# Delta rule in a hybrid block: 32x32 blocks joined by single block products; norm roots and two gate outputs moved on ScalarE

## The reference

```python
u = rms_norm(h)
proj = einsum(u, w_in)            # attention q,k,v; delta q,k,v; out-gate; beta; decay; two branch gates
y_a = differential_attention(...) # per-head RMSNorm of the result
# delta rule, per chunk and head, A strictly lower triangular:
A = where(strict, einsum('bhnid,bhnjd->bhnij', k * beta, k) * decay, 0)
T = inverse(I + A)                # unit lower triangular solve against I
v_new = T @ (v * beta) - (T @ (k * beta * exp(gc))) @ S
o = (q * exp(gc)) @ S + (q @ k.T * decay) @ v_new
S = S * g_tot + k_dec.T @ v_new
y_d = rms_norm(o) * silu(gate)
mixed = sigmoid(gate_a) * (y_a @ w_branch_attn) + sigmoid(gate_d) * (y_d @ w_branch_dn)
h = h + mixed @ w_out
h = h + hierarchical_moe(rms_norm(h))   # 32 experts, top-1 group, top-2 experts
out = rms_norm(h)[meta:]
```

## Time and profile before

| | |
|---|---|
| median of 3 runs | 659.19 us (658.57 to 659.19) |
| profiled execution: its own time | 658.39 us |
| profiled execution: span | 656.7 us |
| granted TensorE clock, mean | 0.968 |
| TensorE busy | 601.6 us (92%) |
| VectorE busy | 326.4 us (50%) |
| ScalarE busy | 267.8 us (41%) |
| GpSimd busy | 55.2 us (8%) |

### The profile page before, as it was taken

How to read it: one execution, slowest core, us unless ns; L and a number is a source line. 1 busy time by engine, 2 the same in 40 slices (tenths; PEclk the granted TensorE clock), 3 DMA queues, 4 the chain that set the end, 5 groups by cost and what they waited for, 6 DMA issues and landing times.

```text
span 656.7 us, 14323 instructions
## 1 busy us (share of the span) xinstructions
PE 601.6 (92%) x5931; PEld 505.6 (77%) x5931; DVE 326.4 (50%) x693; ACT 267.8 (41%) x598; POOL 55.2 (8%) x102
## 2 busy tenths in 40 slices
PE   8999999999999799999999999999999778686985
PEld 8999999989998788999899999997554533444551
DVE  5344467888877558465756389534122111110103
ACT  6245566777778545324533575423110010000103
POOL 8300011110000002100310030000000000000000
PEclk9899999999999899999999999999999988896989
DMA  9745443434335233222421169999999999999993
GB/s 289 242 146 179 151 144 99 138 119 135 122 126 191 66 129 130 66 66 65 130 66 66 65 225 347 420 422 416 421 421 419 421 422 423 422 422 421 421 405 129
DMA packets 68560, 156.04 MB, mean 238 GB/s; under 512 B 4818, under 2 KB 54116, under 8 KB 56596
## 3 DMA queue, kind: packets, MB, share of 16 engines
q1 hardware_dynamic: 67136, 154.89, 62.7%
q0 software_dynamic: 176, 0.17, 0.2%
q10 hardware_dynamic: 1188, 0.12, 0.2%
HBM read 154.12 MB, written 1.05 MB: 236 GB/s over the span
## 4 chain that ended last, share of the span: by engine, by line
PE 67%; DMA 8%; DVE 8%; SPq 7%; ACT 6%; issue 3%; ACTq 0%; DVEq 0%
PE bank L861 33%; DMA arena<-in_expert_w_gate_dram 8%; PE bank L1272 7%; SPq L526 7%; PE bank L1048 5%; PE bank L846 3%; PE bank L1297 2%; PE bank L1253 2%; PE bank L1026 2%; PE bank L1308 2%; DVE ring_lo L341 1%; PE bank L929 1%; ACT w_hi L336 1%; DVE arena L1921 1%; ACT arena L1572 1%
## 5 line engine op out<-in xcount | busy, mean ns | idle before, releaser
L861 PE MATMUL bank<-uT_hi,w_hi 128*128 128x272 f32 (+1 forms) x568 | 169.5, 298 | 3.4 <-ACT arena L1441 3.4
L861 PE MATMUL bank<-uT_hi,ring_lo 128*128 128x272 f32 (+1 forms) x568 | 163.4, 288 | 0.0
L861 PE MATMUL bank<-uT_lo,w_hi 128*128 128x272 f32 (+1 forms) x568 | 163.3, 288 | 0.0
L341 DVE TENSOR_TENSOR ring_lo<-arena,w_hi 128x1024 fp32r<-128x1024 f32 x88 | 107.6, 1225 | 49.0 <-ACT w_hi L336 48.8
L861 PEld LDWEIGHTS bank<-uT_hi,w_hi 128*128 128x128 f32 x568 | 108.6, 191 | 6.2 <-ACT w_hi L336 3.9
L861 PEld LDWEIGHTS bank<-uT_lo,w_hi 128*128 128x128 f32 x568 | 108.7, 191 | 0.2 <-issue 0.2
L861 PEld LDWEIGHTS bank<-uT_hi,ring_lo 128*128 128x128 f32 x568 | 108.6, 191 | 0.0
L336 ACT ACTIVATE w_hi<-arena 128x1024 fp32r<-128x1024 f32 x88 | 92.0, 1051 | 0.9 <-DMA arena<-in_w_in_dram 0.9
L1272 PE MATMUL bank<-arena 128*32 128x256 f32 x1024 | 67.6, 423 | 20.9 <-DMA arena<-in_expert_w_gate_dram 20.9
L1272 PEld LDWEIGHTS bank<-arena 128*32 128x32 f32 x1024 | 35.5, 121 | 47.8 <-issue 26.9
L1921 DVE SCALAR_TENSOR_TENSOR arena<-arena 128x272 f32<-128x272 f32 x72 | 35.9, 498 | 12.3 <-ACT arena L1434 11.6
(11 more groups left out here) (368 smaller groups left out, 1011.7 us busy)
## 6 DMA issues: line engine op xcount, KB each, us to landing
arena<-in_w_in_dram SPq DMA_DIRECT2D x36, 1024.0 KB, 5.2
arena<-in_expert_w_gate_dram SPq DMA_DIRECT2D x32, 1024.0 KB, 24.9
arena<-in_expert_w_up_dram SPq DMA_DIRECT2D x32, 1024.0 KB, 21.8
arena<-in_expert_w_down_dram SPq DMA_DIRECT2D x29, 1024.0 KB, 22.0
arena<-in_w_branch_attn_dram SPq DMA_DIRECT2D x4, 1024.0 KB, 5.2
arena<-in_w_branch_dn_dram SPq DMA_DIRECT2D x4, 1024.0 KB, 5.1
arena<-in_w_out_dram SPq DMA_DIRECT2D x4, 1024.0 KB, 8.3
arena<-in_expert_w_down_dram SPq DMA_DIRECT2D x6, 512.0 KB, 18.3
```

Source lines behind the costliest of these rows:

```text
L341: nc.vector.tensor_tensor(low_of(SPLIT[q]), src, w_hi[HI_OF[q]].bitcast(F32), ALU.subtract).then_inc(w_lo_ready, 1)
L861: last = pe.matmul(ps[:, 0:b.shape[2]], a[:, c, :], b[:, c, :], start=(c == 0 and i == 0), stop=(c == NC - 1 and i == 2))
```

## The change

In the delta rule, each joined pair of 32x32 blocks is now one product of 32x32 blocks, in its own tile of the array. x2 multiplies A's blocks straight from `w[1]` by T's block, the result going to the rows of the lower block (tiles (0,32) and (64,96), 8 products per chain); VectorE multiplies it by the key factor on its way out of PSUM (it was ScalarE's copy). t2 makes the lower product for rows 32 to 63 in tile (32,32), and the two transposed ones in tiles (32,0) and (96,64), 12 products per chain; VectorE copies three 32x32 blocks for the four heads to their places. ScalarE copies T's transposed diagonal to `w[0]` in t1. GpSimd's mask `off64_c` and its multiply go.

On ScalarE, `roots` follows `key_roots` at once, with the table load left at its old place behind the first meta step; and the outputs of the first two gate tiles in the mix (gate+2, gate+3) stand ahead of the splits beside them, on VectorE too.

```diff
{DIFF}
```

More of the change, by code:

```diff
@@ L17 @@
 Q = P // 2
+B = P // 4
 META = 16
@@ L129, in hybrid_block @@
         block16 = new(P)
-        ident_c, block16_c, off32_c, off64_c = (new(Q) for _ in range(4))
+        ident_c, block16_c, off32_c = (new(Q) for _ in range(3))
+        new(Q)
         tri16, causal_add16, spread16 = (new(P) for _ in range(3))
@@ L459, in diagonal, with rows32 @@
             return a[q * Q:(q + 1) * Q, :, q * Q:(q + 1) * Q]
+        def rows32(i):
+            return slice(i * B, (i + 1) * B)
         every, first_half, rest = slice(None), slice(0, H // 2), slice(H // 2, H)
@@ L489, in hybrid_block @@
                     BEHIND.append(("split", n))
+                elif steps_seen == 1:
+                    BEHIND.insert(-1, ("tile", n))
                 else:
@@ L701, in _ @@
                     link(pool.memset(off32_c[half, 32 * b:32 * b + 32], 1.0))
-                link(pool.tensor_scalar(off64_c[rows, :], off32_c[rows, :], -1.0, 1.0, ALU.mult, ALU.add))
                 link(pool.tensor_tensor(off32_c[rows, :], off32_c[rows, :], block16_c[rows, :], ALU.subtract))
@@ L764, in dn @@
                     wait_dn(pool, "act", t, c, "at")
-                    pool.tensor_tensor(small(c, 4, 0), small(c, 6, 1), off32_c.unsqueeze(1).broadcast_to([P, 4, Q]), ALU.mult)
-                    pool.tensor_tensor(small(c, 4, 1), small(c, 6, 1), off64_c.unsqueeze(1).broadcast_to([P, 4, Q]),
+                    pool.tensor_tensor(small(c, 4, 0), small(c, 6, 1), off32_c.unsqueeze(1).broadcast_to([P, 4, Q]),
                                        ALU.mult).then_inc(dn_pool[c], 1)
@@ L1041, in dn, with both @@
                 Xs, Ys, Zs = (bank[2 + 3 * c + i][:, 0:4 * Q].rearrange("p (h i) -> p h i", h=4) for i in range(3))
-                def both(o, lhsT, rhs, quarters=(0, 1)):
+                def both(o, lhsT, rhs):
                     for h in range(n):
-                        for q in quarters:
+                        for q in range(2):
                             rows = slice(q * Q, (q + 1) * Q)
@@ L1121, in dn @@
                     need("dve", "t32")
-                    both(Zs, small(c, 4, 1), T)
+                    for h in range(n):
+                        for i in (0, 2):
+                            pe.matmul(Zs[rows32(i + 1), h, 0:B], w[1][rows32(i), h, rows32(i + 1)], T[rows32(i), h, 0:B], start=True, stop=True,
+                                      tile_position=(i * B, (i + 1) * B))
                     last = each(Y, kT, lambda h: S[:, 4 * c + h, :])
                 elif s == "t2":
-                    need("act", "x2")
-                    both(Zs, TT_, X_, (0,))
-                    last = both(Xs, X_, TT_)
+                    need("dve", "x2")
+                    for h in range(n):
+                        pe.matmul(Zs[rows32(1), h, 0:B], TT_[rows32(1), h, B:Q], X_[rows32(1), h, 0:B], start=True, stop=True,
+                                  tile_position=(B, B))
+                        for i in (1, 3):
+                            last = pe.matmul(Xs[rows32(i - 1), h, 0:B], X_[rows32(i), h, 0:B], TT_[rows32(i), h, B:Q], start=True, stop=True,
+                                             tile_position=(i * B, (i - 1) * B))
                 elif s == "x3":
@@ L1531, in roots @@
                 act.activation(rs_halves, rs_rows, ACT.Copy).then_inc(rs_ready, 1)
-                act.preload_act_table_set("exp_and_others")
             for m in range(FIRST_SLOT, SLOTS_A):
@@ L1595, in dn @@
                         done(act.activation(small(c, 5, 1), Xs, ACT.Copy))
-                elif s == "x2":
-                    wait_dn(act, "pe", t, c, s)
-                    done(act.activation(small(c, 5, 0), Zs, ACT.Copy))
+                elif s == "t1":
+                    wait_dn(act, "dve", t, c, "t32")
+                    for q in range(2):
+                        last = act.activation(diagonal(w[0], q), small(c, 5, 1)[q * Q:(q + 1) * Q], ACT.Copy)
+                    done(last)
                 elif s == "v":
@@ L1617, in _ @@
             key_roots()
+            roots()
             for what, arg in BEHIND:
                 if what == "roots":
-                    roots()
+                    act.preload_act_table_set("exp_and_others")
                 elif what == "split":
@@ L2064, in dn @@
                     of_pe()
+                    done(tt(piece(5, 0)[:, :, 0:B], Zs[:, :, 0:B], per_head(nbk, B), ALU.mult))
                     for h in range(n):
@@ L2069, in dn @@
                     of_pe()
-                    tt(T[0:Q], Zs[0:Q], T[0:Q], ALU.add)
-                    for q in range(2):
-                        rows = slice(q * Q, (q + 1) * Q)
-                        last = tt(diagonal(b(0), q), Xs[rows], piece(5, 1)[rows], ALU.add)
+                    dve.tensor_copy(T[rows32(1), :, 0:B], Zs[rows32(1), :, 0:B])
+                    wait_dn(dve, "act", t, c, "diag")
+                    for i in (0, 2):
+                        last = dve.tensor_copy(b(0)[rows32(i), :, rows32(i + 1)], Xs[rows32(i), :, 0:B])
                     done(last)
```

4 lines of the change are left out of this document (2 added, 2 removed).

## The result

The kernel with the change takes **655.55 us** (median of 16 runs, 649.6 to 657.3), the one before, on the same chip, 658.83 us (median of 16, 654.84 to 663.05). The ratio is 0.9942, with the interval 0.9919 to 0.9966; it lies near the ratio of the two means (0.9944), and that of the two medians would be 0.9950. The profiled execution took 656.16 us, its span is 654.4 us: 2.2 and 2.3 less than those of before.

What follows compares the result with a forecast made beforehand. The expert weight stream bounds the kernel from 392 us, and earlier TensorE savings start it sooner. From 658.39 us, less 0.5 (stall) and 1.8 (products), 656.1; with the median 0.8 higher, 656.9 us, range 654.9 to 659.1.

Steps and rivals of the forecast that it cites:

- The bound, and where a saving counts: From 392 us the expert weight stream sets the pace; TensorE time saved before about 390 us comes off one for one.
- product term: Smaller products in x2 and t2 of the delta rule, four times in all, save 1.8 us on TensorE's path.
- The stall: Before gate+4, about 217 us: wait falls from 3.36 to 0.6 us, 2.7 us returns before s2; 0.5 us kept.
- Rival 4: The stall before gate+4 goes altogether as VectorE reaches L2023 in time; 653.0 us, chance 0.04.
- The clock: Behind the stall the clock likeliest falls again to 1.2 GHz, costing about 1.6 us as before, so no term.
- the middle between 1.1 and 2.5: Saving on x2 and t2 taken as 1.8 us, between a 30.6 ns pass floor (1.1) and continued column scaling (2.5).
- the two products of rows 32 to 63 go one after another: In t2, these take 16 passes at 31 ns, 0.49 us, the third product beside them; 0.51 us saved against 1.0.
- the upper end: In x2 and t2 time goes with the columns: 0.24 and 0.51 us saved, times four 3.0 us.
- rival 3: In x2 and t2 the 32x32 tiles stop overlapping, 3.1 us lost; 661.8 us in all, chance 0.1.
- Rival 2: In x2 and t2 narrower products are no cheaper, only the stall's 0.5 us stays; 658.7 us, chance 0.16.
- Edits at nothing: Copies and multiplies moved or added on ScalarE, VectorE and GpSimd in x2, t1 and t2 cost TensorE nothing.
- The sum: Whole kernel: profiled 658.39 us less 0.5 and 1.8 is 656.1; with the median 0.8 higher, 656.9 us.

Runs made afterwards that it cites:

- e3_s1_first: The changed kernel with the meta chunk's s1 moved ahead of the splits on ScalarE, VectorE and GpSimd; 653.66 us, ratio 0.993 to the kernel before.
- e5_by_tile: The changed kernel with t2's products ordered tile by tile, four heads in each, instead of taking the tiles in turn; one run, 656.19 us.
- e9_alternate: The kernel before with t2's three 64x64 products head by head, tile (64,64) between the two of tile (0,0); t2 2.00 us as before, span 659.4 us.
- e7_again: The changed kernel, unchanged, profiled a second time; one run, 650.94 us.
- e6_compact: The changed kernel with s1 and s2 moved early and all products of delta-rule steps s1 to t1 made as 32x32 blocks; 659.26 us, ratio 1.0009 to before.

## Why the prediction was right, and where it was not

**The bound, and where a saving counts: right.** (One row was misread: 20.9 us is what TensorE's four waits for gate weights take together, the longest is 6.5 us. The bound is the same.) The stretch at 415 GB/s kept its length, the stream began 4.35 us earlier, and the leads at `t2` and behind it were kept up to 390 us. The time of 655.55 us lies inside the range. It is 1.35 us below the forecast of 656.9, about the 0.2% that a measurement tells. The main reason is the product term, which was 1.9 us short.

**The stall: right in place and size.** Gate+4 was forecast at 217.63 with 0.6 us of idle time and stood at 217.52 with 0.52. L2039 (before: L2023) was forecast at 221.24 and started at 221.07, `s2` at 221.72 and started at 221.34. The term was 0.5 us, and the trace gives 0.9 at `s2` and 0.6 at chunk 0. `e3_s1_first` shows that the cause was VectorE's order: with `s1` ahead of the splits the wait at `s2` is gone. Rival 4, by which the whole stall of 3.4 us goes, failed on just this.

**The clock: right in price, not a matter of one answer.** The fall costs 1.5 us, where 1.6 was taken. The step "the likeliest case has the clock fall again" held in the changed kernel's first profile and failed in its second, so that taking one of the two was a guess that the first profile happened to bear out. I had taken idle time as what decides. It doesn't alone: 0.52 and 2.16 us of it went both ways.

**The product term was mis-sized: 1.8 us taken, 3.7 measured.** The step that failed is the choice of the middle between 1.1 and 2.5, and within the bounds the sentence "the two products of rows 32 to 63 go one after another". For `x2` the upper end was exact: 0.24 us saved per chain. A pass of 32x32 blocks holds its tile for 31 ns, so the time in a tile does go with the columns from 128 (111 ns) to 64 (60) to 32 (31). For `t2` I gave the rows 32 to 63 to one pass at a time. They are two tiles, (32,32) and (32,0), and all three tiles ran beside each other: 0.63 us for both chains instead of 1.0 at my upper end. The real upper end was four times 0.24 and twice 1.37. I had seen that the two products now differ in their columns of the array, and used it only for the bad side, in rival 3.

**The rivals on the product.** Rival 2 (no cheaper) and rival 3 (tiles stop overlapping) are both refuted by 0.37 and 0.63 us. `e5_by_tile` shows that overlap is worth 0.5 us per chunk, and `e9_alternate` that it can't be had without the smaller blocks. The Trainium skill's rule in "TensorEngine Tiling (Array Packing)", on instruction overhead, of about 60 cycles for each matmul, by which rival 2 would have held, doesn't agree with this trace if it is read in columns: passes in one tile go from about 60 ns to 31 as the columns halve. Read as a time, 60 cycles at the 2.4 GHz level are 25 ns by an estimate, less than either, and the trace doesn't speak against it within a tile. The floor of about 25 ns between small matmuls, in the Trainium skill's "TensorE: Matmul & The Clock Gate", the part on the back-to-back issue gap, doesn't hold across tiles here: 48 passes in 0.63 us are 13 ns each, and within a round they start 7 ns apart. In one tile they start 31 ns apart, above it.

**Edits at nothing: right.** ScalarE's four copies in `t1` (1.71 us from 280.33) ended at 282.04 and L1453 started at 282.06, against 282.37 for L1441; all of it has moved 0.6 us earlier, so the pairs delayed it by some 0.3 us and TensorE didn't notice. A pair took 0.86 us, where I had put 0.64. VectorE's new multiply took 0.29 us, and its copies in `t2` 0.28 us each. TensorE shows no wait for any of them.

**The sum.** By the terms as measured, 3.7 and 0.6, and with the same base of 659.19, it would have been 654.9; the measured ratio's interval, on 658.83, is 653.5 to 656.6. The forecast of 656.9 lies 0.3 us outside it. The 0.6 us holds with the clock fallen as in before; where it stays up, as in `e7_again`, TensorE is 1.5 us further ahead. As 654.9 is the range's lower end, it took some luck that the result lies inside it.

## What to carry to other kernels

Where small products stand on the path, look for blocks of zeros in them: a product cut down to its 32x32 blocks cost half the time of a 64x64 one in its tile, and tiles that share rows but not columns still ran side by side, if the order takes them in turn. But count the instructions: the same cut applied to all steps, with twice the instructions in them, left TensorE idle for 10.1 us with nothing awaited that the profile shows, and took the whole gain. And when a wait is taken away by moving one engine's work, read on that engine's timeline what stands in front of the next operand. Here the gain of 2.8 us at one tile was 0.9 us one step later, and it took more moves, on three steps, to keep it.

## What the runs showed of the hardware that I had not expected

- Tiles (32,32) and (32,0) of the array, the same rows with different weights, overlap in the changed kernel: rounds of three passes start about 31 ns apart, 13 ns per pass over `t2`.
- Passes in different tiles start out of the order of the program. In `e5_by_tile`, L1140's first pass starts at 287.13, after five of the eight passes of L1136 that stand ahead of it. In the changed kernel's `t2` one pass of L1136 and two of L1139 alternate, so it seems that a product's second pass comes after the first passes of its neighbours.
- TensorE can idle with nothing awaited in a dense run of small products: 10.1 us in seven pieces in `e6_compact`, the longest 3.3 us, each ending 2.4 to 2.8 us after an instruction packet starts. (That it had run out of instructions is inferred.)
- The same two idle pieces, 0.52 and 2.16 us, were followed by a fall to the 1.2 GHz level in one execution of the same program and not in the other, with a difference of 1.5 us by chunk 0. What else decides is open.
- In the tail the clock fell in some profiles and made 16 products last 3.65 us instead of 1.97. No experiment tried to keep it up.
